# A four-layer transformer kernel: three weight blocks side by side, k-tile by k-tile, behind each norm

## The reference

```python
h = modulate(rms_norm(x, norm1_g[i]), sh1, sc1)      # first norm; y*(1+scale)+shift
z = h @ w_in[i]                                      # 1024 -> 2048, then norms of q and k, rope, attention
x = x + g1 * (concat([out_a, out_b, out_c]) @ w_out[i])
h = modulate(rms_norm(x, norm2_g[i]), sh2, sc2)      # second norm
a = conv1d(h @ w_up[i]) + conv_b                     # 1024 -> 5632, taps along the tokens
x = x + g2 * ((silu(gate) * val) @ w_down[i])        # 2816 -> 1024
```

## Time and profile before

| | us |
|---|---|
| median of 3 runs | 1854.69 (1851.66 to 1856.66) |
| the profiled execution: its span, first to last instruction | 1861.0 |
| TensorE busy | 1728.0 |
| VectorE busy | 992.2 |
| ScalarE busy | 827.3 |
| GpSimd busy | 159.2 |

### The profile page before, as it was taken

One profiled execution on the slowest core, in us unless ns is written; L12 is line 12 of the kernel. 1 busy time (PEld: TensorE's weight loads), 2 busy tenths in 40 slices (PEclk: granted clock), 3 DMA queues, 4 the chain that ended last, 5 costly groups with the idle time before them and its releaser, 6 DMA issues.

```text
span 1861.0 us, 31505 instructions
## 1 busy us (share of the span) xinstructions
PE 1728.0 (93%) x11096; PEld 1442.8 (78%) x11096; DVE 992.2 (53%) x1737; ACT 827.3 (44%) x1442; POOL 159.2 (9%) x238
## 2 busy tenths in 40 slices
PE   4999899899999999998999999989889999579997
PEld 2787686567777766665967899988689999579997
DVE  3333863544444432224575688666446664666654
ACT  3323672433333322223355566544455554445543
POOL 0250000011111111110500000001000000000000
PEclk9999999899999999998999899999998999679999
DMA  9554002356656656663320366553124556325554
GB/s 369 203 179 173 1 1 91 123 200 211 225 211 218 212 181 220 220 226 138 114 79 1 124 181 181 166 168 124 36 69 136 181 164 181 95 80 181 181 160 121
DMA packets 85040, 285.08 MB, mean 153 GB/s; under 512 B 9408, under 2 KB 12736, under 8 KB 84448
## 3 DMA queue, kind: packets, MB, share of 16 engines
q1 hardware_dynamic: 58528, 187.31, 31.6%
q0 software_dynamic: 26432, 96.68, 15.1%
HBM read 282.90 MB, written 1.05 MB: 153 GB/s over the span
## 4 chain that ended last, share of the span: by engine, by line
PE 85%; DVE 9%; ACT 2%; DMA 2%; issue 1%; POOL 1%; SPq 0%; DVEq 0%; ACTq 0%; POOLq 0%
PE B L1415 21%; PE B L1417 20%; PE B L1416 20%; PE B L1441 6%; PE B L1585 3%; PE B L1615 3%; PE B L1462 2%; DVE NORM L1003 2%; PE B L1603 1%; PE B L1477 1%; DVE HL L993 1%; PE B L1428 1%; PE B L1430 1%; PE B L1429 1%; DVE SM L1060 1%
## 5 line engine op out<-in xcount | busy, mean ns | idle before, releaser
L1415 PE MATMUL B<-HH,WHI 128*128 128x256 f32 (+1 forms) x1872 | 613.9, 328 | 46.7 <-DVE HL L993 25.0
L1417 PE MATMUL B<-HH,WLO 128*128 128x256 f32 (+1 forms) x1872 | 596.2, 318 | 0.0
L1416 PE MATMUL B<-HL,WHI 128*128 128x256 f32 (+1 forms) x1872 | 595.9, 318 | 0.0
L921 DVE TENSOR_TENSOR WLO<-RAW,WHI 128x1024 fp32r<-128x1024 f32 (+1 forms) x376 | 413.0, 1102 | 280.1 <-ACT WHI L562 279.3
L562 ACT ACTIVATE WHI<-RAW 128x1024 fp32r<-128x1024 f32 (+1 forms) x376 | 358.9, 959 | 269.8 <-PE B L1417 269.7
L1415 PEld LDWEIGHTS B<-HH,WHI 128*128 128x128 f32 x1872 | 363.4, 194 | 128.1 <-issue 82.5
L1417 PEld LDWEIGHTS B<-HH,WLO 128*128 128x128 f32 x1872 | 364.0, 194 | 23.4
L1416 PEld LDWEIGHTS B<-HL,WHI 128*128 128x128 f32 x1872 | 365.1, 195 | 18.8
L1415 PE MATMUL B<-MIDH,WHI 128*128 128x256 f32 (+1 forms) x704 | 222.9, 317 | 0.0
L1417 PE MATMUL B<-MIDH,WLO 128*128 128x256 f32 (+1 forms) x704 | 219.2, 311 | 0.0
L1416 PE MATMUL B<-MIDL,WHI 128*128 128x256 f32 (+1 forms) x704 | 218.9, 311 | 0.0
(11 more groups left out here) (174 smaller groups left out, 1783.9 us busy)
## 6 DMA issues: line engine op xcount, KB each, us to landing
RAW<-in_wup SPq DMA_DIRECT2D x176, 512.0 KB, 3.7
GW<-in_wmod POOLq DMA_DIRECT2D x136, 512.0 KB, 4.4
RAW<-in_wdn SPq DMA_DIRECT2D x64, 384.0 KB, 3.2
RAW<-in_wproj SPq DMA_DIRECT2D x44, 512.0 KB, 4.4
RAW<-in_wdn SPq DMA_DIRECT2D x64, 320.0 KB, 3.3
RAW<-in_wout SPq DMA_DIRECT2D x24, 512.0 KB, 3.8
GWD<-in_wmod POOLq DMA_DIRECT2D x24, 512.0 KB, 4.2
MW<-in_wmod SPq DMA_DIRECT2D x4, 2048.0 KB, 18.3
```

The costliest lines, as they stand in the source:

```text
L921: v.tensor_tensor(WL[s][:, 0:kts, :], RAW[s][:, 0:kts, :], WH[s][:, 0:kts, :].bitcast(F32), ALU.subtract).then_inc(lo_done, 1)
L1415: mm(bank[:, 0:t], wh, a, start=first and k == 0, stop=False)
L1416: mm(bank[:, 0:t], wh, b, start=False, stop=False)
L1417: ins = mm(bank[:, 0:t], wl, a, start=False, stop=stop and k == kts - 1)
```

## The change

Behind seven norms (the first ones of layers 0 to 2, the second ones of all four layers) the first three blocks are no longer computed one after the other. `products_by_kt` goes over the k-tiles, and at each k-tile over blocks 0, 1 and 2, each in a bank of its own; a block whose split is made within the norm joins at a later k-tile and catches up there. The splits move: `in_norm` names the k-tile behind which ScalarE and VectorE split a block. In the first norm of layer 0 these are block 1 behind k-tile 0, block 2 behind k-tile 2, block 3 behind k-tile 7; in the other first norms block 2 behind k-tile 1 and block 3 behind k-tile 7; in the second norm of layer 0 the same, of layer 1 block 2 behind k-tile 2. In the second norms of layers 2 and 3 all three are split before. The loop of `w_up` is written out once more in TensorE's program, since its first pass now differs.

```diff
@@ norm, ScalarE (VectorE's has lo_split in the same places)
                     ins.then_inc(nh_ready, 1)
+                    if kt in in_norm(key):
+                        n = in_norm(key)[kt]
+                        hi_split(n // 4, n % 4, block_kts(n))
@@ the order of pairs
+        def side_by_side(key):
+            n0 = (BASE if key[1] == "n1" else UP0)[key[0]]
+            joins = {n - n0: kt + 1 for kt, n in in_norm(key).items()}
+            done, order = [0, 0, 0], []
+            for kt in range(KT):
+                for b in range(3):
+                    if kt >= joins.get(b, 0):
+                        order += [(b, k) for k in range(done[b], kt + 1)]
+                        done[b] = kt + 1
+            return order
@@ TensorE
+            def products_by_kt(key, tokens):
+                n0 = (BASE if key[1] == "n1" else UP0)[key[0]]
+                base = norm_count[ROUND[key]]
+                seen = set()
+                for b, k in side_by_side(key):
+                    pe.wait_ge(nl_ready, base + k + 1)
+                    if b not in seen:
+                        pe.wait_ge(lo_done, n0 + b + 1)
+                        seen.add(b)
+                    s, t = (n0 + b) % 4, tokens[b]
+                    mm(banks[b][:, 0:t], WH[s][:, k, :], HH[:, k, 0:t], start=k == 0, stop=False)
+                    mm(banks[b][:, 0:t], WH[s][:, k, :], HL[:, k, 0:t], start=False, stop=False)
+                    ins = mm(banks[b][:, 0:t], WL[s][:, k, :], HH[:, k, 0:t], start=False, stop=k == KT - 1)
+                    if k == KT - 1:
+                        ins.then_inc(blk_used, 1)
@@ proj, TensorE
                 for i in range(NSLOT[l]):
-                    if i < TPROJ[l]:
+                    if i == 0:
+                        products_by_kt((l, "n1"), [proj_tokens(l, TILES[l][b]["name"]) for b in range(3)])
+                    if 3 <= i < TPROJ[l]:
@@ w_up, TensorE
                 def body(i, last):
                     n4 = UP0[l] // 4 + i
+                    first = isinstance(i, int) and i == 0
+                    if first:
+                        pe.wait_ge(drained, TUP0[l])
+                        products_by_kt((l, "n2"), [t] * 3)
                     for s in range(4):
-                        pe.wait_ge(lo_done, 4 * n4 + s + 1)
-                        pe.wait_ge(drained, TUP0[l] + 4 * i + s - 3)
-                        products(s, 8, banks[s], t, ready=(nl_ready, nbase) if s == 0 else None).then_inc(blk_used, 1)
+                        if not first or s == 3:
+                            pe.wait_ge(lo_done, 4 * n4 + s + 1)
+                            pe.wait_ge(drained, TUP0[l] + 4 * i + s - 3)
+                            products(s, 8, banks[s], t).then_inc(blk_used, 1)
                         if l == 0:
                             c = 14 + 2 * i + s // 2
-                loop(pe, FT // 2, body)
+                loop(pe, FT // 2, body, peel=True)
```

More of the change, by code:

```diff
@@ L399, in after_norm, with in_norm @@
             l, which = key
-            if key in ((0, "n2"), (1, "n2"), (2, "p1")):
+            if key == (2, "p1"):
                 return [UP0[l] + 2, UP0[l] + 3]
-            if which == "p2" and l < 3 or which == "n1" and l in (1, 2):
-                n = BASE[l + (which == "p2")]
-                return [n + 2, n + 3]
+            if which == "p2" and l < 3:
+                return [BASE[l + 1] + 2, BASE[l + 1] + 3]
             return []
+        def in_norm(key):
+            l, which = key
+            if key == (0, "n1"):
+                return {0: 1, 2: 2, 7: 3}
+            if key == (0, "n2"):
+                return {1: UP0[0] + 2, 7: UP0[0] + 3}
+            if key == (1, "n2"):
+                return {2: UP0[1] + 2, 7: UP0[1] + 3}
+            if which == "n1" and l in (1, 2):
+                return {1: BASE[l] + 2, 7: BASE[l] + 3}
+            return {}
+        def side_by_side(key):
[8 more added lines that the diff above has]
+            return order
         def stats_done(r):
@@ L884, in _ @@
                 norm((l, "n1"))
-                if l == 0:
-                    for s in (1, 2, 3):
-                        hi_split(0, s, 8)
                 if l < 3:
@@ L996, in lo @@
                     ins.then_inc(nl_ready, 1)
+                    if kt in in_norm(key):
+                        n = in_norm(key)[kt]
+                        lo_split(n // 4, n % 4, block_kts(n))
                 for kt in range(KT):
@@ L1378, in _ @@
                 norm((l, "n1"))
-                if l == 0:
-                    for s in (1, 2, 3):
-                        lo_split(0, s, 8)
                 if l < 3:
@@ L1496, in proj @@
                 names = qk_names[l]
-                base = norm_count[ROUND[l, "n1"]]
                 col, _, _ = scols[l]
@@ L1537, in proj @@
                         pe.wait_ge(lo_done, n + T["blocks"])
-                        if i >= 3:
-                            pe.wait_ge(drained, TBASE[l] + i - 2)
+                        pe.wait_ge(drained, TBASE[l] + i - 2)
                         if T["qs"] is None:
-                            ins = products(n % 4, 8, bank, proj_tokens(l, T["name"]),
-                                           ready=(nl_ready, base) if i == 0 else None)
+                            ins = products(n % 4, 8, bank, proj_tokens(l, T["name"]))
                         else:
@@ L1695, in body @@
                             chunk_part(c, [0, 1] if s % 2 == 0 else [2, 3], "mid")
-                nbase = norm_count[ROUND[l, "n2"]]
-                loop(pe, FT // 2, body)
+                loop(pe, FT // 2, body, peel=True)
                 if l == 0:
```

## The result

| | before | after |
|---|---|---|
| median of 9 runs each, us | 1855.5 (1851.66 to 1864.12) | 1871.88 (1865.45 to 1878.45) |
| ratio, 95% interval | | 1.0089 (1.0067 to 1.0110) |
| span of the profiled execution, us | 1861.0 | 1876.7 |

The account below looks back on a forecast made before the run. TensorE was taken as the bound, busy 1728.0 of 1861.0 us. Gains of 3.8 us and losses of 4.0 left the span at 1861 and the median, 6.3 below it, at 1855 us; range 1848 to 1863.

Parts of the forecast that it names:

- Part 1: Side by side in the norms: TensorE no longer starves except in the very first; small second norms gain 0.45, 0.5, 0.5.
- Part 2: Moved splits: later k-tiles come 1.2 us later, hidden by TensorE's backlog, except in the first norm, with a 1.3 us wait.
- third bullet of Part 3: Layer 0's second norm: idling 4.4 and 3 us halves the clock over most of block 3, 2.4 us more, 3.8 late in all.
- the first bullet: `proj`, first norms of layers 1 and 2: second column sums wait for ScalarE's root; block 3 still gains 1.75 and 0.6.
- The sum: Whole kernel: gains of 3.8 us against losses of 4.0, so a span of 1861 again and a median of 1855.
- the fourth bullet: Layer 0's first norm: four ring buffers, so one round of loads counts; block 3 at 70.3 against 70.07, 0.2 late.
- The ring in layer 0 dominates: Rival, layer 0's second norm: load rounds of 6 to 7.4 us, block 4 10 late; about 6 slower, 1861; chance 0.20.
- Turning through three banks: Rival, side-by-side pairs: changing banks slows matmuls to half-clock pace, over 50 us slower, past 1900; chance 0.03.
- Nothing moves: Rival, every norm: the three blocks' followers cost what the side by side gave; counted inside the forecast, no chance of its own.
- the prediction's bounds: Layer 0's second norm: loads of 3.6 to 7.4 us put block 4 0.2 to 7 late; clock costs 0 to 3.4.

Follow-up runs that it names:

- e1: Side by side, splits within the norm, only behind layer 0's first norm, all else as in the kernel before: 1860.49 us, ratio 1.0018.
- e2: Side by side only behind layer 0's second norm, all else as in the kernel before: 1865.66 us, ratio 1.0044.
- e4: Side by side only behind the second norms of layers 1, 2 and 3, else as in the kernel before: 1853.06 us, ratio 0.9997.
- e3: Side by side only behind the first norms of layers 1 and 2, else as in the kernel before: 1859.22 us, ratio 1.0013.
- e5: e3 plus seven matmuls of unused result ahead of the second column sums, where TensorE waited for the root: 1854.1 us, ratio 0.9992 to the kernel before.
- e6: e3 with block 3's products set ahead of the second column sums: 1856.26 us, ratio 0.9987 to the kernel before.
- e8: e3 with only blocks 0 and 1 side by side, block 2 and its split behind them: 1854.13 us, ratio 0.9988 to the kernel before.
- e9: e1 plus seven matmuls of unused result ahead of the late pair of units: 1860.42 us, ratio 1.0015 to the kernel before.
- e10: Side by side in all norms but layer 0's, block 3 halved between column sums in layers 1 and 2's first norms: 1853.65 us, ratio 0.9975 to before.
- e7: e2 plus 20 and 11 matmuls of unused result ahead of the two later pairs of units: 1864.76 us, ratio 1.0030 to the kernel before.

## Why the prediction was wrong

Part 1 held for the norms of 512 tokens. The end of the three blocks was sized right in layers 0 and 1 (20.8 us after T0 in e1 for 20.4, 18.9 in e2 for 18.8, 18.4 for 18.15), and TensorE did not starve behind the third k-tile. In the small norms the profiled executions differ by 0.49, 0.21 and nothing for the 0.45, 0.5 and 0.5 of the forecast; since unchanged code varies by more, the 0.49 is as well luck, and e4 leaves the 1.45 in all neither shown nor excluded. Part 2 held: no row in these norms waits for VectorE behind the second k-tile.

**The step that failed first is the third bullet of Part 3, "This idle time can cost the clock as well".** It was applied only to the 4.4 us and 3 us of layer 0's second norm, and there to block 3. The gaps of 1.2 us in layer 1 and 1.5 in layer 2 were priced in the first bullet as waits, with block 3 behind them at full clock, although had already shown a fall behind a stretch that was still busy 0.57 of 2.00 us. The sum therefore read the gain at the start of block 3; at the start of block 4 it was gone. By the ratios of e1 to e4, each good to 3 or 4 us, the forecast missed by 4.8 us here (2.35 gained forecast, 2.4 lost), by 4.4 in layer 0's second norm (3.8 and 8.2), by 3.1 in its first (0.2 and 3.3) and by 0.9 in the small norms.

| norm | forecast, us | measured at block 3 | at block 4 | what was mis-sized |
|---|---|---|---|---|
| layer 1, first | 1.75 early | 1.2 early | 0.2 (after) to 1.5 (e3) late | clock, 2.8 in e3 |
| layer 2, first | 0.6 early | 0.1 to 0.4 late | 2.2 to 2.8 late | clock, 2.7 in e3 |
| layer 0, first | 0.2 late | 3.1 to 3.2 late | 3.7 to 5.3 late | waits 1.5 in e1, units apart 1.0, clock 1.4 |
| layer 0, second | 3.8 late | 8 late | 8 to 10 late | the base, 3.4; see below |

Layer 0's first norm: the second load landed later than the fourth bullet had it (its unit could start 7.5 us behind the three blocks in e1 instead of 6.1), the bullet left out that two units that do not arrive together cannot run together, and it took no clock for these waits. In e1 the clock costs the 1.4 us above; in the profiled execution of the changed kernel it is at 0.50 from 78 to 84, over most of block 3, and block 4 is 1.6 us later still.

Layer 0's second norm: block 4 was forecast 2.4 us of clock behind 392.1, at T0 + 42.0, and came at 43.02 in e2 and 45.01 after. That is 1 to 3 us off, and it is partly luck. Block 3 was forecast at T0 + 33.1 and came at 36.20 and 37.28, largely since the half clock lay over units (up to 1.92 us each) that the forecast had at full clock; and in e2 block 3 then ran at full clock, where the forecast had taken 2.4 us more:

```profile
395.00:399.00 4.00, 4.00 (x20) 3.28 (x19) 0.00 (x0) 0.00 (x0) 0.33 (x1) 1.00 0.74 250
```

The two errors nearly cancel. The larger error is in what it was compared with. The profiled execution of before has block 4 at T0 + 38.27; in the seven of e1, e3, e5, e6, e8, e9 and e10, whose code is the same there, it is 34.27 to 35.59. (e4, which has the same code too, reads 38.28.) From that T0 to the first product of layer 1's first norm the execution of before takes 513.30, those seven 506.03 to 506.94 and e4 511.86. So the row I took as the normal state was 3.4 us late at block 4. The loads of the units are what differs: those issued in the 11 us behind the second pair of units took 5.2 and 5.3 us to landing in the median and up to 7.4 in before and e4, and 4.0 to 4.3 in the median in the seven, so that in before the units at 379.65 and 389.75 come late. The text notes that its span lies 6.3 us above the median, and does not ask where. Against the usual 34.9, the same forecast of the changed kernel would have been 7.1 late and not 3.8, and the total 3.3 higher, 1858.

The rivals: "The ring in layer 0 dominates" was nearest (layer 0's second norm costs 8.2 of 16.4 us) and by the right mechanism, two rounds of about 5 us, though not by slow loads: in the changed kernel those issued between 391 and 401 took 4.4 to 4.6, not over 6.5. Its 1861 was still 11 too low, as it kept the 3.8 of gains. "Turning through three banks" is refuted by e5 and e10. "Nothing moves", because the followers cost what the side by side gave, is the right mechanism in layers 1 and 2, but the followers cost more than was given. The Trainium skill, page TensorE: Matmul & The Clock Gate, section HAM oscillation, cited beside the step, describes bursts between DMA waits; the trace agrees at 391.31 (0.50 from 388 on, within the wait of 4.96 us), and shows the same behind ScalarE's root at 902.55, a wait that is no DMA and 1.19 us long.

One sum of the prediction's bounds is off as well: two rounds at 3.6 and at 7.4 us in place of 4.3 put block 4 of layer 0's second norm between 0.0 and 7.6 late, not 0.2 and 7.

What stays open: why the first product stands at different times, and why those loads land late in some executions of the same code. The clock's share in e2 is between 0 (at the next norm) and 0.8 us (at block 4) by e7. No run tried a larger ring.

## What to carry to other kernels

Work that is made dense in one place completes its results together, and what follows them then queues: read the followers' engine in its own order and look for a hole between small matmuls. A hole of 0.5 to 1.5 us there can cost more in clock than in waiting, though it does not in every case; read the gain one whole block behind the edit, not at its seam, and put half a block of real products into the hole. Before trusting a row of one profiled execution as the base of a term, ask where that execution differs from the median.

## What the runs showed of the hardware

- The clock fell behind or within gaps of 0.46 us (e6, layer 1), 0.45 (e8, both layers), 1.19 and 1.20 (after and e3, layer 1) and 1.50 and 1.51 (after and e3, layer 2), each between groups of eight matmuls with one to four output columns. It did not fall behind 0.45 in e6, layer 2, where a group of four follows. In e10 the same groups between halves of a block of products saw no fall.
- Among wide matmuls longer idle time passed without a fall. Before, TensorE is idle 0.42, 0.61 and 0.61 us ahead of k-tiles of layer 1's first norm, at a granted clock of 1.00 from 870 to 875, and 1.40 us ahead of the unit at 389.75, with 1.00 from 389 to 391. So the length of a gap alone does not decide. One such row before:

```profile
871.96 0.50 PE L1415 MATMUL B<-HH,WHI 128*128 128x512 f32 x1 [0.61 <-DVE HL L993]
```

- At full clock a unit (matmuls on 32 columns of the array) takes 1.05 us alone, and two units issued together take 1.07 (e7 at 378.20, after at 385.28), so units whose loads land 0.6 us apart cost 1 us more than the wait shows. The Trainium skill, page TensorEngine Tiling (Array Packing), section Key Properties, says that different tiles of the array can execute weight loads and matmuls in parallel; the trace agrees, with 1.07 us for two units in place of 2.10.
